# Chunk-band attention on one core: values as the stationary operand, two heads side by side in the array's column halves

## What is computed

```python
def band_attend(q, kb, vb, bias, key_valid):
    s = jnp.einsum('bnthd,bnmhd->bnhtm', q, kb).astype(jnp.float32) * (HEAD_DIM ** -0.5)
    s = s + bias.astype(jnp.float32)[None, None]
    s = jnp.where(key_valid[None, :, None, None, :], s, NEG_INF)
    p = jax.nn.softmax(s, axis=-1).astype(vb.dtype)
    return jnp.einsum('bnhtm,bnmhd->bnthd', p, vb)
```

## Time and profile before

| what | value |
|---|---|
| median of 3 runs | 2694.84 us (2688.36 to 2695.31) |
| span of the profiled execution, first to last instruction | 2692.3 us |
| what the median has beyond that span | 2.5 us |
| attention stage | about 768 to 1074 us of the span |
| PE busy over the span | 98% |
| mean granted TensorE clock | 0.992 |
| the chain that ended last: PE / DVE / ACT / DMA | 84% / 5% / 4% / 3% |

### The profile page before, as it was taken

The page is one execution under the profiler, slowest core; times in us unless marked ns, Lnnn a source line. Parts: engine busy times, 40 slices in busy tenths (PEclk is TensorE's granted clock), DMA queues, the critical chain, the costliest instruction groups (busy, mean ns, idle before and its releaser), DMA issues.

```text
span 2692.3 us, 50625 instructions
## 1 busy us (share of the span) xinstructions
PE 2645.6 (98%) x18664; PEld 1771.5 (66%) x18664; DVE 1750.8 (65%) x3367; ACT 1362.9 (51%) x2666; POOL 628.2 (23%) x698
## 2 busy tenths in 40 slices
PE   7999999999999999999999999999999999999998
PEld 2466666666668888557996666666666666666665
DVE  4966464655646666776778788888888875242433
ACT  4967474755656666113556555565555653121211
POOL 2600000000008889000000254433344311101000
PEclk9999999999999999999999999999999999999999
DMA  8621322031294442556552354445545438567572
GB/s 281 200 74 66 135 78 105 25 109 71 93 231 95 112 156 105 183 210 202 143 142 69 126 181 166 171 168 189 181 159 179 165 120 325 212 233 262 210 249 106
DMA packets 238419, 423.07 MB, mean 157 GB/s; under 512 B 57816, under 2 KB 162776, under 8 KB 230056
## 3 DMA queue, kind: packets, MB, share of 16 engines
q1 hardware_dynamic: 229400, 412.03, 46.1%
q10 hardware_dynamic: 8848, 8.74, 1.0%
HBM read 283.42 MB, written 139.92 MB: 157 GB/s over the span
## 4 chain that ended last, share of the span: by engine, by line
PE 84%; DVE 5%; ACT 4%; DMA 3%; issue 2%; POOL 1%; SPq 0%; DVEq 0%; ACTq 0%; POOLq 0%
PE ps L2988 57%; PE ps L3240 14%; PE ps L3080 4%; PE ps L3067 3%; PE ps L3056 2%; DMA arena<-in_w_mod_rest 2%; PE ps L2912 1%; ACT arena L1600 1%; PE ps L3094 1%; POOL arena L1140 1%; PE ps L3029 1%; DVE arena L2393 1%; DVE arena L2471 1%; ACT arena L1607 1%; DVE arena L2089 0%
## 5 line engine op out<-in xcount | busy, mean ns | idle before, releaser
L2988 PE MATMUL ps<-arena 128*128 128x352 f16 (+1 forms) x11880 | 1613.1, 297 | 5.1 <-ACT arena L1768 2.1
L2988 PEld LDWEIGHTS ps<-arena 128*128 128x128 f16 x11880 | 1100.6, 97 | 513.1 <-ACT arena L1768 2.5
L3240 PE MATMUL ps<-arena 128*128 128x352 f16 x2772 | 414.9, 310 | 0.5 <-DVE arena L2689 0.5
L3240 PEld LDWEIGHTS ps<-arena 128*128 128x128 f16 x2772 | 264.7, 96 | 150.8 <-issue 1.0
L1197 POOL TENSOR_TENSOR arena<-arena 128x128 f32<-128x128 f32 x44 | 30.6, 695 | 740.4 <-DMA arena<-in_w_down 740.1
L3094 PE MATMUL ps<-arena 128*128 128x424 f16 (+1 forms) x960 | 172.5, 341 | 2.1 <-DVE arena L2471 1.4
L1760 ACT ACTIVATE arena<-ps 128x352 f32<-128x352 f32 x264 | 116.3, 460 | 98.8 <-PE ps L2988 98.8
L1153 POOL CAST arena<-arena 64x512 f16<-64x512 f32 x8 | 4.9, 610 | 689.6 <-DMA arena<-in_cache_kT 689.3
L3080 PE MATMUL ps<-arena 128*128 128x64 f32 (+2 forms) x1200 | 151.0, 272 | 0.5 <-DVE arena L2435 0.5
L1207 POOL TENSOR_TENSOR arena<-arena 128x176 f32<-128x176 f32 (+1 forms) x57 | 56.2, 986 | 398.4 <-DMA arena<-ffn_hidden 398.4
L3080 PEld LDWEIGHTS ps<-arena 128*128 128x128 f32 (+2 forms) x1200 | 144.4, 193 | 3.4 <-issue 2.1
(11 more groups left out here) (239 smaller groups left out, 3587.1 us busy)
## 6 DMA issues: line engine op xcount, KB each, us to landing
hidden_combinations<-arena SPq DMA_DIRECT2D x48, 616.0 KB, 3.2
arena<-hidden_combinations SPq DMA_DIRECT2D x24, 1232.0 KB, 7.8
arena<-in_w_up SPq DMA_DIRECT2D x44, 512.0 KB, 4.9
down_combinations<-arena SPq DMA_DIRECT2D x44, 448.0 KB, 2.8
ffn_hidden<-arena SPq DMA_DIRECT2D x44, 440.0 KB, 3.1
arena<-down_combinations SPq DMA_DIRECT2D x10, 1792.0 KB, 7.8
arena<-down_combinations SPq DMA_DIRECT2D x20, 896.0 KB, 6.9
arena<-ffn_hidden SPq DMA_DIRECT2D x50, 352.0 KB, 3.9
```

Of the source, the lines that this page charges most:

```text
L2988: mm = pe.matmul(out, wt[:, k, wp, :], act_t[:, k, hp], start=(first and k == 0 and n == 0), stop=(last and k == K - 1 and n == 2), skip_g ...
L3240: mm = pe.matmul(ps[:, down_bank(n, k), 0:CF].rearrange("p (w t) -> p w t", w=2), dwt(i)[:, wi, wp, :], dact[i][:, :, bi, hp, :], start=(i ...
```

## The change

It does six things.

1. `outs` works on a tile, not on a unit: the values are the stationary operand (64 columns) and the transposed probabilities the moving one (128 columns). Head 0 writes output partitions 0 to 63 and head 1 partitions 64 to 127, so their matmuls lie in the two column halves of the array, taken in turn. The result comes out transposed, in banks 6 and 7 by turns. A tile's chunks are done in two parts, one in each of two steps: three and two chunks for a wide tile.
2. The transpose of the output (`out_t`, its semaphore `ot_filled`) goes.
3. The row sums, one number for each query, have to lie along the row now: `sums` multiplies them, broadcast to 64 stationary columns, with the identity, once for each head, into unused columns of bank 1.
4. DVE takes the reciprocal of that 128x128 block (`inverse_sums`) right after its `scores`, in place of two reciprocals of 128x1. `out_n` multiplies two 128x128 blocks once for each tile, in place of two 128x64 multiplications. ACT's and DVE's split into f16 parts reads `osb` from SBUF.
5. `pt`, `sm` and the reciprocals get two buffers each; ACT's `probs` and `exps` get one more wait each.
6. PE's step becomes `sums` (odd steps), `scores`, a part of `outs`, `probs`, and the output comes two steps later. The first product of the merge moves behind the loop. SP's waits count tiles.

The core of the diff:

```diff
+            def sums(x):
+
+                pe.wait_ge(p_ready, x.u + 2)
+                keep_above_zero(pe, s_added, min(x.u + 3, NU - 1))
+                keep_above_zero(pe, r_ready, x.tile)
+                for h in range(2):
+                    mm = pe.matmul(sum_cols[64 * h:64 * h + 64, 0:x.rows],
+                                   sm[0:x.rows, x.tile % 2, h:h + 1].to_broadcast([x.rows, 64]),
+                                   ident[0:x.rows, 0:x.rows], start=True, stop=True)
+                mm.then_inc(r_filled, 1)
+
+            def outs(x, part):
+
+                if x.i == 0 and part == 0:
                     pe.wait_ge(values_loaded[x.b], x.b + 1 + 48 * (x.j // 2) + 48)
-                pe.wait_ge(t_act, x.u + 1)
-                keep_above_zero(pe, t_dve, wide(x.u + 1))
-                keep_above_zero(pe, o_ready, x.u)
+                if part == 0:
+                    pe.wait_ge(t_act, x.u + 2)
+                    keep_above_zero(pe, t_dve, wide(x.u + 2))
+                    keep_above_zero(pe, o_ready, x.tile - 1)
                 nk = (x.w + P - 1) // P
-                for c in range(nk):
+                half = (nk + 1) // 2
+                for c in (range(half), range(half, nk))[part]:
                     k = min(P, x.w - c * P)
-                    mm = pe.matmul(ps[0:x.rows, 6, 64 * x.h:64 * x.h + 64], pt[0:k, x.h, c * P:c * P + x.rows],
-                                   vv[x.b][0:k, x.v0 + c, 64 * x.h:64 * x.h + 64],
-                                   start=(c == 0), stop=(c == nk - 1))
-                mm.then_inc(o_filled, 1)
-
-            def out_t(x):
-                pe.wait_ge(o_ready, 2 * x.tile + 2)
-                keep_above_zero(pe, ot_ready, x.tile)
-                pe.transpose(ps[:, 7, 0:P], osb, ident).then_inc(ot_filled, 1)
+                    for h in range(2):
+                        mm = pe.matmul(out_cols(x.tile)[64 * h:64 * h + 64, 0:x.rows],
+                                       vv[x.b][0:k, x.v0 + c, 64 * h:64 * h + 64],
+                                       pt[x.tile % 2][0:k, h, c * P:c * P + x.rows],
+                                       start=(c == 0), stop=(c == nk - 1), skip_group_check=True)
+                if part == (nk > 1):
+                    mm.then_inc(o_filled, 1)
...
-            for g in range(-1, NU + 3):
+            for g in range(-1, NU + 4):
+                if g % 2 == 1 and 3 <= g < NU + 3:
+                    sums(Unit(g - 3))
                 if g + 1 < NU:
                     scores(Unit(g + 1))
...
+                if g >= 4:
+                    outs(Unit((g - 4) // 2 * 2), g % 2)
                 if 0 < g <= NU:
                     probs(Unit(g - 1))
-                if 1 < g <= NU + 1:
-                    outs(Unit(g - 2))
-
+
+            pe.wait_ge(mix_loaded, 16 * NJ)
+            pe.wait_ge(d_split, 1)
+            pe.wait_ge(s_added, NU)
+            pe.wait_ge(r_ready, NTILE)
+            merge_product(0, 1)
```

DVE and ACT:

```diff
+            def inverse_sums(x):
+                dve.wait_ge(r_filled, x.tile + 1)
+                keep_above_zero(dve, o_ready, x.tile - 1)
+                dve.reciprocal(orec[x.tile % 2][:, 0:x.rows], sum_cols[:, 0:x.rows]).then_inc(r_ready, 1)
...
-                dve.tensor_scalar(osb[0:rows, 64 * h:64 * h + 64], ps[0:rows, 6, 64 * h:64 * h + 64],
-                                  rs[0:rows, h:h + 1], None, ALU.mult).then_inc(o_ready, 1)
+                dve.tensor_tensor(osb[:, 0:x.rows], out_cols(x.tile)[:, 0:x.rows], orec[x.tile % 2][:, 0:x.rows], ALU.mult)\
+                    .then_inc(o_ready, 1)
...
-            for g in range(NU + 3):
+            for g in range(NU + 7):
                 if g < NU:
                     scores(Unit(g))
+                if g % 2 == 0 and 4 <= g < NU + 4:
+                    inverse_sums(Unit(g - 4))
                 if 0 < g <= NU:
                     probs(Unit(g - 1))
-                if 1 < g <= NU + 1:
-                    out_n(Unit(g - 2))
-                if g % 2 == 0 and g >= 4:
-                    out_lo(Unit(g - 4))
+                if g % 2 == 0 and g >= 8:
+                    out_lo(Unit(g - 8))
+                if g % 2 == 0 and 6 <= g < NU + 6:
+                    out_n(Unit(g - 6))
```

```diff
             def exps(x):
                 act.wait_ge(s_added, x.u + 1)
+                keep_above_zero(act, r_filled, x.tile - 1)
...
                 act.wait_ge(t_filled, x.u + 1)
+                keep_above_zero(act, o_filled, x.tile - 1)
...
-                if g % 2 == 0 and g >= 4:
-                    out_hi(Unit(g - 4))
+                if g % 2 == 1 and g >= 7:
+                    out_hi(Unit(g - 7))
```

More of the change, by code:

```diff
@@ L164, in build @@
         pr = at_(45120, 2 * BAND).rearrange("p (h n) -> p h n", h=2)
-        pt = at_(46400, 2 * BAND).rearrange("p (h n) -> p h n", h=2)
-        osb = at_(47680, P)
-        mark, least, sm, rs = (at_(47808 + 2 * i, 2) for i in range(4))
+        pt = [at_(o, 2 * BAND).rearrange("p (h n) -> p h n", h=2) for o in (46400, 51776)]
+        osb, orec = at_(47680, P), [at_(o, P) for o in (53056, 53184)]
+        mark, least = (at_(47808 + 2 * i, 2) for i in range(2))
+        sm = at_(47812, 4).rearrange("p (b h) -> p b h", b=2)
         crow = at_(13056, 2 * D)
@@ L335, in build @@
         o_ready = sem("o_ready")
-        ot_filled = sem("ot_filled")
+        r_filled = sem("r_filled")
         ot_hi = sem("ot_hi")
@@ L483, in build, with out_cols @@
         NU = NUNIT * NJ
+        NTILE = NU // 2
+        def out_cols(t):
+            return ps[:, 6 + t % 2, 0:P]
+        sum_cols = ps[:, 1, P:2 * P]
         def wide(n):
@@ L1599, in exps @@
                 act.wait_ge(s_added, x.u + 1)
+                keep_above_zero(act, r_filled, x.tile - 1)
                 act.activation(pr[0:x.rows, x.h, 0:x.w], pr[0:x.rows, x.h, 0:x.w], ACT.Exp, scale=-1.0,
-                               bias=least[0:x.rows, x.h:x.h + 1], accum_out=sm[0:x.rows, x.h:x.h + 1]).then_inc(p_ready, 1)
+                               bias=least[0:x.rows, x.h:x.h + 1],
+                               accum_out=sm[0:x.rows, x.tile % 2, x.h:x.h + 1]).then_inc(p_ready, 1)
             def probs(x):
                 act.wait_ge(t_filled, x.u + 1)
+                keep_above_zero(act, o_filled, x.tile - 1)
                 m = min(4, (x.w + P - 1) // P)
-                act.activation(pt[:, x.h, 0:m * P], ps[:, 4, 0:m * P], ACT.Copy).then_inc(t_act, 1)
+                act.activation(pt[x.tile % 2][:, x.h, 0:m * P], ps[:, 4, 0:m * P], ACT.Copy).then_inc(t_act, 1)
             def out_hi(x):
-                act.wait_ge(ot_filled, x.tile + 1)
-                act.activation(mixT[:, x.j, 0, x.q0:x.q0 + x.rows], ps[:, 7, 0:x.rows], ACT.Copy, scale=XS).then_inc(ot_hi, 1)
+                act.wait_ge(o_ready, x.tile + 1)
+                act.activation(mixT[:, x.j, 0, x.q0:x.q0 + x.rows], osb[:, 0:x.rows], ACT.Copy, scale=XS).then_inc(ot_hi, 1)
             def merge_hi(f):
@@ L1656, in merge @@
                         .then_inc(m_stored[1], 16)
-            for g in range(NU + 3):
+            for g in range(NU + 6):
                 if 0 < g <= NU:
@@ L2417, in probs @@
             def probs(x):
[L2419 to L2422, removed]
                 if x.w > 512:
@@ L2425, in probs @@
                     dve.wait_ge(t_filled, x.u + 1)
-                    dve.tensor_copy(pt[0:k, h, 4 * P:5 * P], ps[0:k, 5, 0:P]).then_inc(t_dve, 1)
-            def out_n(x):
[L2430 to L2434, removed]
-                dve.tensor_scalar(osb[0:rows, 64 * h:64 * h + 64], ps[0:rows, 6, 64 * h:64 * h + 64],
-                                  rs[0:rows, h:h + 1], None, ALU.mult).then_inc(o_ready, 1)
+                    keep_above_zero(dve, o_filled, x.tile - 1)
+                    dve.tensor_copy(pt[x.tile % 2][0:k, x.h, 4 * P:5 * P], ps[0:k, 5, 0:P]).then_inc(t_dve, 1)
+            def inverse_sums(x):
+                dve.wait_ge(r_filled, x.tile + 1)
+                keep_above_zero(dve, o_ready, x.tile - 1)
+                dve.reciprocal(orec[x.tile % 2][:, 0:x.rows], sum_cols[:, 0:x.rows]).then_inc(r_ready, 1)
+            def out_n(x):
+                dve.wait_ge(o_filled, x.tile + 1)
+                dve.wait_ge(r_ready, x.tile + 1)
+                keep_above_zero(dve, ot_ready, x.tile)
+                dve.tensor_tensor(osb[:, 0:x.rows], out_cols(x.tile)[:, 0:x.rows], orec[x.tile % 2][:, 0:x.rows], ALU.mult)\
+                    .then_inc(o_ready, 1)
             def out_lo(x):
@@ L2440, in out_lo @@
                 dve.wait_ge(ot_hi, x.tile + 1)
-                dve.scalar_tensor_tensor(mixT[:, x.j, 1, t], ps[:, 7, 0:x.rows], XS, mixT[:, x.j, 0, t],
+                dve.scalar_tensor_tensor(mixT[:, x.j, 1, t], osb[:, 0:x.rows], XS, mixT[:, x.j, 0, t],
                                          ALU.mult, ALU.subtract).then_inc(ot_ready, 1)
@@ L3050, in scores @@
                 keep_above_zero(pe, s_added, x.u - 1)
+                if x.h == 0:
```

(1 more changed line is left out.)

14 lines of the change are left out of this document (2 added, 12 removed).

## The result

The changed kernel takes 2705.74 us (median of 9 runs, 2701.11 to 2709.26); the kernel before, run beside it, 2695.14 us. The ratio is 1.0038, 95% interval 1.0027 to 1.0049: slower by 0.4%. The forecast was 2706 us. The number is right. The account behind it is wrong in its largest term (15 us for TensorE's odd steps) and in one that it put at nothing (VectorE's work), and the errors cancel by luck. The trace shows this at once.

The account below looks back on a forecast made before the run. PE and ACT were taken as level in a 2.27 us ring; +14.9, -1.6, -1, +2 and -3 made about +11 us on the span of 2692.3, so 2703.6, plus 2.5 for the median: 2706 us, range 2689 to 2753.

Parts of the forecast that it names:

- The ring: Transposes, ACT's copy, ACT's next exponential, transposes again: a loop of 2.27 us that sets a wide unit's pace.
- the room in it: The 1.77 us between one unit's last transpose starting and the next transposes, for all other PE work of a step.
- Passages of 0.10 us: On PE, each change between 128 and 64 weight columns leaves the array standing still for about 0.10 us.
- The odd step's 0.31 us over: PE's odd step needs 2.08 us, 0.31 too much, so the unit takes 2.58; 48 wide tiles give +14.9 us.
- The clock: Rival: half-wide products bring the granted clock of 0.50 everywhere, about +1.1 us a unit, over 2800 us; chance 0.04.
- DVE and the split: DVE's 0.95 us reciprocal costs nothing, with 0.1 us of cover; output product and split each last about 0.28, the copy's time.
- The passages between sets: At three places between sets, spreading the sample's products over two steps gains 1 us each, -3 us in all.
- Faster, by the passages between sets: Rival: odd steps fit and three passages between sets lose their whole 3.1 us each, some 2684 us; chance 0.11.
- wide units: In the attention stage: +14.9 for odd steps, -1.6 for the dropped output transpose, -1 for slow first units.
- narrow units: Narrow tiles, two a set outside the passage between sets, exceed their shorter ring: 8 x 0.27, +2 us.

Follow-up runs that it names:

- after_split_from_psum: The changed kernel with the reciprocal's product written back to its PSUM bank and both parts of the split read from there: 2681.52 us, ratio 0.9953.
- after_psum_sums_behind: The changed kernel with the split reading PSUM, and also the sums placed behind the scores of their step: 2681.05 us, ratio 0.9948.
- before_pool_short: The kernel before with GpSimd's adaLN products and sums cut to 8 or 16 columns: 2692.93 us, ratio 0.9997.
- before_sbuf_pool_short: The kernel before with ACT's extra copy to SBUF, DVE's split reading that, and GpSimd's adaLN instructions cut to 8 or 16 columns: 2694.93 us, ratio 1.0003.
- after_pool_short: The changed kernel with GpSimd's adaLN products and sums cut to 8 or 16 columns: 2682.17 us, ratio 0.9962.
- psum_halves_apart: The changed kernel with the split reading PSUM and the output products' head and chunk loops exchanged: 2687.16 us, ratio 0.9974.

## Why the forecast was right, and where it was wrong

*The ring, and the room in it:* right. Even units take 2.26 us, and PE waits for the exponential there. In after_split_from_psum the pace is 2.26 and 2.30 to 2.31 again, and in after_psum_sums_behind, where PE has less to do in odd steps, it is 2.26 in both, the length of the ring, and not less.

*Passages of 0.10 us:* right. In the tile above, the last scores start at 953.92 + 0.72 - 0.22 = 954.42 and stream for 0.055, and the output records start at 954.57: 0.10 again.

*The odd step's 0.31 us over:* wrong, the first failed term. The step was "a half's two records follow each other at 0.11 and the four weight loads, 0.058 each, set 0.23 us a chunk", and with it "Four records of 64 weight and 128 moving columns, 0.33 us overlapped". I had let one half begin only behind the other's first record and had put the four loads in a row. In fact both halves load and stream together. `sums` and its passage take 953.92 - 953.55 = 0.37 us from first start to the scores' start; less the first loads (0.05) and the passage (0.10 and 0.02), that leaves about 0.21 for the sums instead of 0.33. Eight output records and the passage take 955.16 - 954.57 = 0.59, so two chunks take 0.43 instead of 0.55. The two differences are 0.24 of the missing 0.28 us, and 48 tiles at +0.31 became 48 tiles at about +0.04.

*The clock:* right for the undisturbed wide stretches. In the unit of 8.64 us it falls in a wide stretch too, to 0.50 (1.2 GHz), after TensorE has waited 4.65 us for DVE's minimum. The windows view gives the busy time of PE, PEld, DVE, ACT and POOL, then the clock:

```profile
1057.00:1063.00 6.00, 5.16 (x27) 3.10 (x28) 3.74 (x11) 2.25 (x5) 5.44 (x7) 0.50 0.00 0
```

*DVE and the split:* wrong, the second failed term and the cause of the result. The prediction said of DVE's work "It costs nothing, with 0.1 us of cover", with a split "about as long as the copy". It priced the instruction by its size alone and did not ask where its operands lie. The reciprocal is as forecast: 0.95 us, starting behind the minimum. The cover that it gave to the next minimum, 0.1 and another 0.9 us, was about right too: the trace has 1.14. It left out that TensorE's next scores wait for the same minimum, with 0.44 us of room. What it had wrong above all is the price of the split. It meets GpSimd and takes 35 us more in the stage, up to 2.2 us more in one step, which is twice the cover. That comes through as 24 us of time, by after_split_from_psum against the changed kernel, of which about 6 are the unit that the merge's product lengthened too. That the diff takes the split's first input from SBUF, and that GpSimd works through most of the stage, were both to be seen before; neither was weighed.

*The passages between sets:* -1 us each was forecast. ACT's timeline at the first of them, in the changed kernel and in after_split_from_psum:

```profile
840.31 0.60 ACT L1617 ACTIVATE arena<-ps 128x512 f32<-128x512 f32 x1 [0.61 <-PE ps L3081]
...
844.84 0.60 ACT L1617 ACTIVATE arena<-ps 128x512 f32<-128x512 f32 x1 [1.59 <-PE ps L3081]
...
847.25 0.28 ACT L1617 ACTIVATE arena<-ps 128x128 f32<-128x128 f32 x1 [1.43 <-PE ps L3081]
```

```profile
837.97 0.60 ACT L1617 ACTIVATE arena<-ps 128x512 f32<-128x512 f32 x1 [0.45 <-PE ps L3080]
...
839.93 0.60 ACT L1617 ACTIVATE arena<-ps 128x512 f32<-128x512 f32 x1 [0.61 <-PE ps L3080]
...
841.37 0.28 ACT L1617 ACTIVATE arena<-ps 128x128 f32<-128x128 f32 x1 [0.29 <-PE ps L3080]
...
842.44 0.28 ACT L1617 ACTIVATE arena<-ps 128x128 f32<-128x128 f32 x1 [0.42 <-PE ps L3080]
```

The earlier trace rows had 7.5 us for the three units behind the sample tile's first copy. With the split in PSUM it is 842.44 - 837.97 = 4.5, the rings' own length as the prediction reckoned them, and so at all three passages, with a granted clock of 1.00. With the slow splits, the single unit from 840.31 takes 4.53 and the clock falls there as well; the three passages of the changed kernel take 8.5, 4.8 and 8.3 us. The clock has a large part in this. The order of the kernel before takes 5.5 us for a passage where the granted clock stays at 1.00, as it does at two of three passages of before_pool_short and at all three of before_sbuf_pool_short. So of the 3 us that a passage gives up, 1 is the order, as forecast, and 2 go with the clock. With the new order and no long splits the clock is 1.00 in all twelve passages of four kernels (after_pool_short, after_split_from_psum, after_psum_sums_behind, psum_halves_apart).

*The rival "Faster, by the passages between sets"* gave 2684 us, if the odd step fits and each passage between sets gives up its 3 us. That is what after_split_from_psum does: 2681.5. The condition that it named (an odd step's passages at under 0.09 us) was not what was met; the odd step fits because the halves overlap better.

So the total came out by luck, by errors of opposite sign. TensorE's part was +15 us in the forecast and about +2 in fact; gains between the sets were 3 us and could be 9; and a term of zero was worth 24. The starts of ACT's copies in after_split_from_psum show the terms without the last one: against the kernel before, wide units -3.7 us (forecast +12.3, by +14.9 - 1.6 - 1), the three passages -9.1 (forecast -3), narrow units +2.5 (forecast +2).

## What to carry over

When an edit moves an operand from PSUM to SBUF, count the SBUF inputs of every DVE instruction that reads it, and look at what GpSimd runs in that stage: a second SBUF input can make a 0.29 us instruction wait out a 2.4 us one. Where it can't be avoided, shorter GpSimd instructions take most of the loss away. In this stage the ring of copies and exponentials kept its 2.26 us whatever TensorE's part was, and a total that agreed with the forecast proved little until the units had been compared one by one.

## What the runs showed of the hardware

- Two matmuls in the two column halves run side by side, f32 with 128 moving columns too: the twelve records of a part take 0.88 us, in six pairs whose starts lie 0.11 us apart (0.16 for the first two). Their weight loads overlap as well: those of the first pair begin 6 ns apart and last 0.13 us each.
- The overlap does not need neighbours in different halves. With all records of one half first, twelve take 1.16 us, not 1.5, and eight take 0.67 us, as by turns: there the first records of the two halves start 13 ns apart, though four stand before the second half's first in the program.
- A DVE instruction with two SBUF inputs (scalar_tensor_tensor, 128x128, f32 and f16) lasted until a GpSimd tensor_tensor under way had ended, and once a GpSimd copy: up to 2.49 us beside GpSimd instructions of 2.4 us, up to 1.43 beside ones of 1.27 us. With one input in PSUM it never passed 0.294 us beside the same work.
